# A 64-byte move of the feed-forward weight ring: distance 128 in place of 192 between the two operands of a matmul

## The reference, cut to what matters

```python
def second_block(x, norm_w, ffn_w_gate, ffn_w_up, ffn_w_down, ...):
    h = x
    for layer in range(DEPTH_2):                       # 2 layers
        nw = norm_w[layer]
        f = swiglu(rmsnorm(h, nw[0]), ffn_w_gate[layer, 0], ffn_w_up[layer, 0], ffn_w_down[layer, 0])
        h = h + FFN_RES_SCALE * rmsnorm(f, nw[1])
        ...                                            # a mixer
        f = swiglu(rmsnorm(h, nw[4]), ffn_w_gate[layer, 1], ffn_w_up[layer, 1], ffn_w_down[layer, 1])
        h = h + FFN_RES_SCALE * rmsnorm(f, nw[5])
    return h
```

## The kernel before, in words

| tensor | address | modulo 256 |
|---|---|---|
| f0_ffn_before_ring (64 bytes) | 101600 | 224 |
| f0_ffn_ring | 101664 | 32 |
| f0_ffn_mixed, f0_ffn_spare | 142624 | 32 |
| f0_ffn_silu, f0_ffn_more, f0_ffn_stats | 150816, 152864, 169248 | 32 |
| u (high, low), right side | 212960, 196576 | 224 |
| f0_ffn_sums, right side | 172000 | 224 |
| weight_pieces | 40160 | 224 |

## Time and profile before

### The profile page before, as it was taken

One profiled execution on the slowest core, in us unless ns is written; L12 is line 12 of the kernel. 1 busy time (PEld: TensorE's weight loads), 2 busy tenths in 40 slices (PEclk: granted clock), 3 DMA queues, 4 the chain that ended last, 5 costly groups with the idle time before them and its releaser, 6 DMA issues. The chain is left out here.

```text
span 3384.5 us, 50693 instructions
## 1 busy us (share of the span) xinstructions
PE 3013.8 (89%) x21350; PEld 2450.6 (72%) x21350; DVE 1667.5 (49%) x1988; ACT 1204.4 (36%) x1818; POOL 371.5 (11%) x255
## 2 busy tenths in 40 slices
PE   6997667887767999998779999999999989799999
PEld 4985553333226998786667998799988865689997
DVE  3237651111117872435355874487532457638853
ACT  3116420000005552334324553455334444435532
POOL 2990001000010000100010000100000006300000
PEclk8998878989987999998789999999999999899999
DMA  6533158999974332121013333233312220223422
GB/s 229 181 97 151 54 241 326 426 426 427 427 321 131 123 115 100 50 87 29 1 33 106 101 112 113 64 111 119 113 56 88 87 64 2 82 68 114 125 94 75
DMA packets 221540, 479.66 MB, mean 142 GB/s; under 512 B 17825, under 2 KB 180092, under 8 KB 207758
## 3 DMA queue, kind: packets, MB, share of 16 engines
q1 hardware_dynamic: 214250, 458.96, 37.6%
q0 software_dynamic: 6912, 16.79, 1.3%
q10 hardware_dynamic: 164, 0.84, 0.1%
HBM read 457.65 MB, written 27.28 MB: 143 GB/s over the span
## 5 line engine op out<-in xcount | busy, mean ns | idle before, releaser
L453 PE MATMUL psum_banks<-u_high,f_ffn_ring 128*128 128x256 f32 (+1 forms) x1408 | 408.6, 290 | 0.9 <-DVE f_ffn_ring L3167 0.9
L454 PE MATMUL psum_banks<-u_low,f_ffn_ring 128*128 128x256 f32 (+1 forms) x1408 | 407.6, 289 | 0.0
L455 PE MATMUL psum_banks<-u_high,f_ffn_ring 128*128 128x256 f32 (+1 forms) x1408 | 407.5, 289 | 0.0
L2095 PE MATMUL psum_banks<-expert_ring,experts_x_t 128*64 128x512 f32 x1024 | 247.0, 640 | 51.0 <-DMA expert_ring<-in_expert_w_up 35.8
L453 PEld LDWEIGHTS psum_banks<-u_high,f_ffn_ring 128*128 128x128 f32 x1408 | 264.7, 188 | 10.2 <-DVE f_ffn_ring L3167 4.3
L454 PEld LDWEIGHTS psum_banks<-u_low,f_ffn_ring 128*128 128x128 f32 x1408 | 267.5, 190 | 6.1 <-issue 0.2
L455 PEld LDWEIGHTS psum_banks<-u_high,f_ffn_ring 128*128 128x128 f32 x1408 | 264.7, 188 | 6.0
L453 PE MATMUL psum_banks<-f_ffn_sums,f_ffn_ring 128*128 128x256 f32 x960 | 267.4, 279 | 0.3 <-issue 0.3
L454 PE MATMUL psum_banks<-f_ffn_sums,f_ffn_ring 128*128 128x256 f32 x960 | 267.3, 278 | 0.0
L455 PE MATMUL psum_banks<-f_ffn_sums,f_ffn_ring 128*128 128x256 f32 x960 | 267.3, 278 | 0.0
L3153 DVE TENSOR_TENSOR f_ffn_ring<-f_ffn_more,f_ffn_ring 128x2048 fp32r<-128x2048 f32 x44 | 100.8, 2292 | 292.7 <-ACT f_ffn_ring L3047 292.7
(11 more groups left out here) (703 smaller groups left out, 7680.7 us busy)
## 6 DMA issues: line engine op xcount, KB each, us to landing
expert_ring<-in_expert_w_gate SPq DMA_DIRECT2D x32, 2048.0 KB, 34.6
expert_ring<-in_expert_w_up SPq DMA_DIRECT2D x30, 2048.0 KB, 34.8
expert_ring<-in_expert_w_down SPq DMA_DIRECT2D x28, 2048.0 KB, 37.2
f_ffn_more<-in_ffn_w_down SPq DMA_DIRECT2D x88, 512.0 KB, 4.4
weight_pieces<-in_ffn_w_gate SPq DMA_DIRECT2D x48, 512.0 KB, 4.8
weight_pieces<-in_ffn_w_up SPq DMA_DIRECT2D x48, 512.0 KB, 6.8
f_ffn_more<-in_ffn_w_gate SPq DMA_DIRECT2D x40, 512.0 KB, 4.9
f_ffn_more<-in_ffn_w_up SPq DMA_DIRECT2D x40, 512.0 KB, 6.8
```

The source lines that it names most:

```text
L453: nc.tensor.matmul(out, lhs.high, rhs.high, start=start, stop=False, skip_group_check=True)
L454: nc.tensor.matmul(out, lhs.high, rhs.low, start=False, stop=False, skip_group_check=True)
L455: return nc.tensor.matmul(out, lhs.low, rhs.high, start=False, stop=stop, skip_group_check=True)
L2095: last = nc.tensor.matmul(k.ps[half, bank, :], self.xt[:, q, half], self.rows_of(n, a, q * HID, HID), start=q == 0, stop=q == KD - 1)
```

## The change

The filler ahead of the ring becomes 64 bytes longer: 128 bytes for each partition in place of 64.

```diff
@@ ffn_products
     with Stage(nc, name) as s:
-        s.sb("before_ring", [P, 16])
+        s.sb("before_ring", [P, 32])
         ring = s.sb("ring", [P, H.RING, 2, H.COLS], F32R)
         sums = s.sb("sums", SUMS_SHAPE, F32R, side="right")
```

## The result

| | before | changed |
|---|---|---|
| median of 14 executions each, us | 3397.43 | 3412.73 |
| lowest and highest, us | 3381.25, 3407.91 | 3408.17, 3416.41 |
| profiled execution: span, us | 3384.5 | 3412.3 |

The changed kernel takes 1.0046 times the time of before, 95% interval 1.0033 to 1.0059: slower by about 15 us, and far steadier (8 us between its lowest and highest time against 27). The forecast was 3370 and an improvement; the time lies inside the range (3362 to 3418), on the side of the rival "128 conflicts always" (3416).

A forecast was written before the change was run, and what follows sets the result against it. TensorE's matmuls were taken to bound the slot stages. The profiled 3386.4 us less 15.0 (f1 and f2 at f0's pace) less 1 (plain) gave 3370.4, put at 3370, with a range of 3362 to 3418 us.

The forecast's parts named there:

- 128 conflicts always: Rival: each weight load and matmul in the slots conflicts, 6.7 ns for each of 6720, 3416 us; chance 0.22.
- What bounds the kernel: Slot stages last as long as TensorE's matmuls, 23% of the span; VectorE has some 35 to 40 us spare in each.
- The parts that were costed at nothing: Instructions, waits, DMAs, writes to the new addresses, and down, whose distance stays 0 at 226.7 ns: cost 0.
- The slots: f0 to f3: 6720 matmuls of 256 columns go from distance 192 to 128, taken at 113.4 ns, saving 15.0 us.
- The draw: Rival: distance does nothing, the pace is a draw at each restart of TensorE's stream, 3371 to 3401 us; chance 0.25.
- Plain: 384 matmuls of 512 columns, at 233.3 ns before, could save 0 to 2.5 us; 1 us was taken.
- four slow stages: Reading of the 3401.17 us median as a run with about four slow slot stages; the profiled 3386.4 us had two.

The follow-up runs named there:

- e16: Against the kernel before: plain weights 96 bytes higher inside the ring, plain at distance 96, slots still at 192; 3384.91 us, ratio 0.9982 (0.9963 to 1.0001).
- e12: Slots at distance 0, each slot matmul using 64 stationary columns in place of 128, half the output partitions left out; 3392.1 us, one execution without a ratio.
- e15: Against the kernel before: plain weights 160 bytes higher inside the ring, plain at distance 32, slots still at 192; 3380.06 us against 3388.14, ratio 0.9980.
- e9: Kernel before, distance 192, with TensorE made to stop twice in each pair of the slots; 3751.3 us, one execution without a ratio.
- e13: Against the kernel before: plain weights 192 bytes higher inside the ring, plain at distance 0, slots still at 192; 3399.21 us, ratio 1.0029 (1.0016 to 1.0043).

## Why the prediction was wrong, point by point

**What bounds the kernel: right.** Every window above has TensorE busy throughout and VectorE at 155 to 158 us, whichever the pace. The parts that were costed at nothing cost nothing: down stayed at 389, no new wait appeared.

**The slots: wrong, and it is the step that failed.** The prediction put 0, 64 and 192 on a circle, took 64 as good and 192 as an edge, and let one arc reach over 128. The rows were right and the interpolation was not. At 96, between 64 and 128, the pace is 120.0 ns, and at 160, between 128 and 192, 118.7. 64 isn't good either: the eight triples at 276 had the rarer of its two paces, which 77 of 80 stretches at 64 with ring and u don't get. The prediction called this evidence thin; it deserved a lower chance than 0.45. The term was put at 0 us over the fast pace and measured 5.3 to 6.7 ns for each of 6720 matmuls: 799.9 us in the slots where 762 were forecast, 38 us. That is nearly the whole way from 3370 to 3412.7.

**The rival "always a conflict": right in its side, near in its price.** 3416 was worked out with 120.1 ns, and 283 ns and windows near 202 us were to be seen in all four stages; the changed kernel has 118.7 ns and 199.4 us in three and 120.1 ns and 201.8 us in the fourth, and a duration of 281. Its other argument, that the point half a circle from a bad distance may be as bad, fits 0 and 128 but isn't a law: 32 and 160, or 96 and 224, differ.

**The draw: half right.** For the kernel before the reading holds, as the stops show. But the distance decides what can be drawn: two paces at 192 with the fast one among them, two slow ones at 128. And a stage at 192 that follows plain unbroken doesn't draw: the step with which plain ends sorts all 24 entries. Nor does an unbroken stream always keep its pace: one start some 40 ns late was enough in f2 of e16.

**Plain: no gain.** 1 us was taken; the 512-column matmuls of f1 run at 233.3 ns at 128 as at 192.

**The median of before as "four slow stages": too simple.** mix_in, proj_out and the other products at 192 have the same two paces, so executions differ by more than f0 to f3. In the later comparisons the kernel before had medians of 3388 to 3393.

**Against the page.** The Trainium skill ("TensorE: Matmul & The Clock Gate", section "Step-by-step: what each phase is for") says that a load of the next weights takes no read bandwidth from the running matmul. The runs disagree with what one would conclude from it for the time. Moving the ring by 64 bytes took the slots from 113.4 or 117.8 ns to 118.7 or 120.0, and in e12, with one moving operand at one distance, halving the load (and the outputs with it) moved three stages from 120.0 to 113.3 ns. Whether it is read bandwidth that the two share, the runs don't show.

## What to carry to other kernels

In this kernel TensorE streams without a break and each matmul has its own weight load, and its pace depends on the distance between moving and stationary operand modulo 256, by up to 6% with 256 columns. In a kernel like it, look at start-to-start times of thousands of matmuls, since a few tell only which of several paces they fell into. Measure every distance before trusting a pattern: here the neighbours of the two places that can be fast are all slow. Where identical stages take different times, look at how each is entered; e15, which moves nothing but the operand of the stage ahead, came out about 8 us (0.2%) under the kernel before. The interval of its ratio, 0.9959 to 1.0000, just reaches 1, so the gain is likely but not certain.

## What the runs showed of the hardware that I had not expected

- A stream holds one of several paces for long: 1680 matmuls at 113.4 or at 117.8 ns, at equal addresses, the choice made in the first few after an entry or a stop, or after a single start some 40 ns late (e16's f2, and the end of three parts in e9).
- The preference is not one of 512 and 256 columns alike: distance 0 is the best for 512 (226.7 ns) and the worst for 256 (120.0). A better plain stage (e13) made the kernel slower.
- Half a load at distance 0 has both 113.3 and 120.0 ns, and at 128 a steady 116.6. What price belongs to which reads stays open, as does what the 233 ns step stands for. Distances that aren't multiples of 32 bytes weren't tried.
